# A decoder step's gate and up projections as seven half-size products, the down projection as a stage of its own

## The reference, cut to what matters

```python
D_FF = ((8 * D_MODEL + 767) // 768) * 256        # 5632
...
    hf = _rmsnorm(x, lp['norm_ffn_g'])
    x = x + (jax.nn.silu(hf @ lp['w_gate']) * (hf @ lp['w_up'])) @ lp['w_down']
...
y_prompt = _rmsnorm(xp, final_norm_g)
```

## Time and profile before

| | |
|---|---|
| median of 3 runs | 3788.56 us (3786.82 to 3789.76) |
| the profiled execution | 3790.81 us, span 3789.1 us |
| busy: TensorE (PE) / DVE / ACT / POOL | 92% / 42% / 25% / 2% of the span |
| TensorE's granted clock, mean | 0.965 of full speed |
| feed-forward stage, from co's end to its last matmul | 2218.5 to 3767.8 us |

### The profile page before, as it was taken

How to read it: one execution, slowest core, us unless ns; L and a number is a source line. 1 busy time by engine, 2 the same in 40 slices (tenths; PEclk the granted TensorE clock), 3 DMA queues, 4 the chain that set the end, 5 groups by cost and what they waited for, 6 DMA issues and landing times. The chain is left out here.

```text
span 3789.1 us, 80680 instructions
## 1 busy us (share of the span) xinstructions
PE 3485.2 (92%) x34315; PEld 3316.3 (88%) x34315; DVE 1591.5 (42%) x2387; ACT 958.4 (25%) x1224; POOL 61.5 (2%) x86
## 2 busy tenths in 40 slices
PE   8999999776688779899989999999999999999997
PEld 8899999544577777899957999999999999999997
DVE  4222444445666666433213344344343333333335
ACT  4111111226343534223113232211211211211213
POOL 0000000000011000000000000000000000000000
PEclk9999999888899999999999999999999999999999
DMA  4798222793000345322273222222222222222222
GB/s 174 278 351 323 97 89 90 297 380 147 23 0 0 124 169 193 118 89 78 96 319 141 99 78 90 90 90 98 81 97 94 86 94 90 90 90 90 90 94 86
DMA packets 97289, 492.70 MB, mean 130 GB/s; under 512 B 11025, under 2 KB 15378, under 8 KB 60994
## 3 DMA queue, kind: packets, MB, share of 16 engines
q1 hardware_dynamic: 92146, 472.67, 33.6%
q0 software_dynamic: 4944, 17.08, 1.2%
HBM read 470.25 MB, written 19.45 MB: 129 GB/s over the span
## 5 line engine op out<-in xcount | busy, mean ns | idle before, releaser
L2228 PE MATMUL ps<-hf_hi,whi_f 128*128 128x260 f32 x2816 | 569.6, 283 | 18.7 <-DVE bulk L2207 7.8
L2228 PE MATMUL ps<-hf_hi,wlo_f 128*128 128x260 f32 x2816 | 569.4, 284 | 0.0
L2228 PE MATMUL ps<-hf_lo,whi_f 128*128 128x260 f32 x2816 | 568.6, 284 | 0.0
L179 ACT ACTIVATE whi_f<-raw 128x2048 fp32r<-128x2048 f32 x132 | 252.7, 1915 | 959.6 <-PE ps L2228 958.5
L2228 PEld LDWEIGHTS ps<-hf_hi,whi_f 128*128 128x128 f32 x2816 | 436.3, 189 | 20.8 <-issue 11.9
L2228 PEld LDWEIGHTS ps<-hf_hi,wlo_f 128*128 128x128 f32 x2816 | 436.2, 189 | 0.0
L2228 PEld LDWEIGHTS ps<-hf_lo,whi_f 128*128 128x128 f32 x2816 | 435.1, 189 | 0.0
L183 DVE TENSOR_TENSOR wlo_f<-raw,whi_f 128x2048 fp32r<-128x2048 f32 x132 | 302.6, 2292 | 148.1 <-ACT whi_f L179 148.1
L2228 PE MATMUL ps<-hid_hi,whi_f 128*128 128x260 f32 x1408 | 284.1, 283 | 0.1
L2228 PE MATMUL ps<-hid_hi,wlo_f 128*128 128x260 f32 x1408 | 283.3, 283 | 0.0
L2228 PE MATMUL ps<-hid_lo,whi_f 128*128 128x260 f32 x1408 | 281.9, 281 | 0.0
(11 more groups left out here) (377 smaller groups left out, 4661.1 us busy)
## 6 DMA issues: line engine op xcount, KB each, us to landing
raw<-w SPq DMA_DIRECT2D x262, 1024.0 KB, 4.8
bulk<-kc SPq DMA_DIRECT2D x128, 512.0 KB, 6.3
page_ring<-vc SPq DMA_DIRECT2D x128, 512.0 KB, 6.0
mem_ring<-mkc SPq DMA_DIRECT2D x8, 2048.0 KB, 18.8
mem_ring<-mvc SPq DMA_DIRECT2D x8, 2048.0 KB, 11.5
qkv<-ev_a POOLq DMA_DIRECT2D x24, 260.0 KB, 2.3
qkv_head<-qkv SPq DMA_DIRECT2D x8, 780.0 KB, 7.6
bulk<-xt SPq DMA_DIRECT2D x4, 1040.0 KB, 11.1
```

The lines of the kernel that those rows point to most:

```text
L179: act.activation(whi[:, u, :], raw[:, u, :], ACT.Copy).then_inc(whi_done, 1)
L2228: mm = pe.matmul(ps[:, 2 * u + s, 0:m], wt[:, wslot, kcol:kcol + 128], t[:, k, a:a + m], start=(first and wt is whi and t is th), stop=(la ...
```

## The change

Three things. First, gate and up of one hidden tile become one product of a 2 x 2 block matrix (rows gate and up, columns the two halves of the 2048 inputs) with a 2 x 2 block matrix of `x` (halves of the inputs, halves of the tokens), made by Strassen's scheme in Winograd's form: 7 products of 128 x 1024 by 1024 x 260 in place of 8. The sums of weight quarters that it needs are made on POOL for each of the 44 hidden tiles, in place in the weight buffer; the sums of `x` quarters are made once on DVE, and all seven `x` operands are split into hi and lo once. The results are put together from the seven products on DVE, with two copies out of PSUM on ACT. Second, each hidden tile is written to DRAM by SP; the down projection becomes a stage of its own with 64 weight blocks (4 passes over the 16 output tiles, with 12, 12, 12 and 8 hidden tiles), which loads and splits the hidden tiles again. `x` is written to DRAM during `co` and read back for it, since the Strassen sums overwrite it. Third, in the attention, `place` moves from the beginning of its turn into the turn before.

```diff
@@ attention: place
-                                if i == 0:
-                                    place(t, hh)
+                                if i == 2 and hh == 0:
+                                    place(t, 1)
+                                elif i == 2 and not final:
+                                    place(t + 1, 0)
...
@@ co: x to DRAM
+                    for k in range(KT):
+                        pool.wait_ge(out_done, c0 + k + 3)
+                        if k >= 2:
+                            pool.wait_ge(x_kept[k % 2], 16 * (k // 2))
+                        pool.dma_start(xsp[k, :, :], x[:, k, :]).then_inc(x_kept[k % 2], 16)
...
@@ gate and up, for hidden tile b of turn t
+            operand = [b11, b21, b12, b22, b22, b11, b21]
+            BANK = (0, 1, 2, 3, 0, 1, 2)
...
+                            pool.tensor_tensor(t0, a21, a22, ALU.add).then_inc(s_made, 1)
+                            pool.wait_ge(s_made, count(t, b, 4, 1))
+                            pool.tensor_tensor(a21, a11, a21, ALU.subtract).then_inc(s_made, 1)
+                            pool.wait_ge(wlo_done, count(t, b, NP, lo0 + 1))
+                            pool.wait_ge(s_made, count(t, b, 4, 2))
+                            pool.tensor_tensor(a11, t0, a11, ALU.subtract).then_inc(s_made, 1)
+                            pool.wait_ge(wlo_done, count(t, b, NP, lo0 + 2))
+                            pool.wait_ge(s_made, count(t, b, 4, 3))
+                            pool.tensor_tensor(a12, a12, a11, ALU.subtract).then_inc(s_made, 1)
...
+                            hi(t, b, 6)
+                            more = not (last and b == 3)
+                            if more:
+                                hi(t, b + 1, 0)
+                            act.wait_ge(E, at(t, b, "z"))
+                            act.activation(sg, z, ACT.Sigmoid).then_inc(sig_done, 1)
+                            if more:
+                                for p in (1, 2, 3):
+                                    hi(t, b + 1, p)
...
+                    def lo(t, b, p):
+                        to = slot(is_first(t, b), p)
+                        dve.wait_ge(whi_done, count(t, b, NP, hi0 + p + 1))
+                        dve.tensor_tensor(to[:, 1, :], quarter(b, p), to[:, 0, :].bitcast(f32), ALU.subtract).then_inc(wlo_done, 1)
...
+                    dve.tensor_tensor(b12, b12, b11, ALU.subtract).then_inc(t_made, 1)
+                    lo(0, 0, 0)
+                    x_lo(0)
...
+                        for n, (wn, xs) in enumerate(((0, xh), (0, xl), (1, xh))):
...
+                            for k in range(QK):
+                                mm = pe.matmul(ps[:, 4 * (b % 2) + BANK[p], 0:HALF], to[:, wn, k * 128:k * 128 + 128], xs[:, p, k, :],
+                                               start=(n == 0 and k == 0), stop=(n == 2 and k == QK - 1))
...
@@ down, a second block of instruction streams
+            HEAD = 3
...
+                        sp.dma_start(bulk[:, KT:KT + HEAD, :], hid[k0:k0 + HEAD, :, :].rearrange("k p n -> p k n")).then_inc(h_in[0], 16)
+                        sp.dma_start(bulk[:, KT + HEAD:KT + n, :], hid[k0 + HEAD:k0 + n, :, :].rearrange("k p n -> p k n"))\
...
+                    for c in range(4):
+                        pe.wait_ge(hl_done, MADE_BY[c + 1] if c else 1)
+                        down(c, c * KT, 0, c == 0)
+                        down(c, c * KT + 1, 1, False)
+                        with pe.Fori(1, KT // 2) as t:
+                            for u in range(2):
+                                down(c, t * 2 + (c * KT + u), u, False)
```

More of the change, by code:

```diff
@@ L37 @@
 FFC = D_FF // 512
+HID = D_FF // 128
 LAM_INIT = 0.8 - 0.6 * math.exp(-0.3 * 0)
@@ L231, in project @@
                     squared=None, tail=None, paged=None, dve_first=None, beside=None, dve_begins=None,
-                    block=None, soft=None):
+                    block=None, soft=None, kept=None):
             j0 = jobs[0]
@@ new lines, in decoder_kernel @@
+        late.close()
+        hid = nc.dram_tensor("hidden", (HID, 128, TOK), f32, kind="Internal").ap()
+        QK = KT // 2
+        QW = QK * 128
+        NP = 7
+        j0 = jobs[0]
+        assert j0 % 2 == 0 and FF0 % 2 == 0 and HID % 2 == 0
+        hi0 = lo0 = FF0
+        pe0 = FF0 + 2
+        raw0 = 16 * (FF0 // 2) + 16
+        s_made, cut, E, sig_done = sem("s_made"), sem("product_copied"), sem("hidden_steps"), sem("sig_done")
+        h_out = [sem("h_out0"), sem("h_out1")]
+        xh_done, xl_done, t_made, scaled = sem("xh_done"), sem("xl_done"), sem("t_made"), sem("x_scaled")
@@ new lines, in decoder_kernel, with count @@
+        ssq_done, ms_done, rms_done = [sem(f"ff_{y}") for y in ("ssq", "ms", "rms")]
+        fin_pe, fin_gain, fin_act, fin_dve, fin_out = [sem(f"fin_{y}") for y in ("pe", "gain", "act", "dve", "out")]
+        s0_ = squares.turn(KT)
+        def count(t, b, per, n):
+            return t * (4 * per) + (per * b + n)
+        STEPS = ("g0", "s2", "a", "g1", "z", "s3", "u1", "q", "qr", "u0", "h")
+        PASSES = [(0, 3), (3, 6), (6, 9), (9, FFC)]
+        TILES = [4 * (e - a) for a, e in PASSES]
@@ new lines, in _, with body @@
+                    turns_of(sp, body)
+                @block.gpsimd
+                def _(pool):
+                    def body(t, last):
+                        for b in range(4):
+                            r = blocks[b % 2]
+                            a11, a12, a21, a22 = r[:, 0, 0:QW], r[:, 0, QW:], r[:, 1, 0:QW], r[:, 1, QW:]
+                            landed(pool, t, b)
+                            if not is_first(t, b):
+                                pool.wait_ge(wlo_done, count(t, b, NP, lo0 - NP + 3))
+                                pool.wait_ge(s_made, count(t, b, 4, 0))
+                            pool.tensor_tensor(t0, a21, a22, ALU.add).then_inc(s_made, 1)
[7 more added lines that the diff above has]
+                            pool.tensor_tensor(a12, a12, a11, ALU.subtract).then_inc(s_made, 1)
+                    turns_of(pool, body)
@@ L2125, in _ @@
                 def _(act):
[L2126 to L2149, removed]
@@ new lines, in _ @@
+                    for i in range(NB):
+                        if i + 2 < NB:
+                            hi(i + 2)
+                        c, k = i // KT + 1, i % KT - 3
+                        if c < 4 and 0 <= k < TILES[c]:
+                            hidden_hi(c, k)
+                        if c == 4:
+                            k = i % KT
+                            act.wait_ge(out_done, j0 + i + 3)
+                            squares.square(act, x[:, k, :], k % 2, s0_ + k)
+                            act.activation(x[:, k, :], x[:, k, :], ACT.Copy, scale=V("g_final", k)).then_inc(fin_gain, 1)
@@ L2224, in _ @@
                 def _(pe):
-                    def product(k, kcol, u, wslot, th, tl, first, last):
-                        for wt, t in ((whi, th), (whi, tl), (wlo, th)):
-                            for s, (a, m) in enumerate(SPANS):
-                                mm = pe.matmul(ps[:, 2 * u + s, 0:m], wt[:, wslot, kcol:kcol + 128], t[:, k, a:a + m],
-                                               start=(first and wt is whi and t is th), stop=(last and wt is wlo))
-                        return mm
```

447 lines of the change are left out of this document (327 added, 120 removed).

## The result

The change makes the kernel slower: 3886.11 us (median of four runs, 3883.86 to 3890.37) against 3788.56, a ratio of 1.026 with a 95% interval of 1.024 to 1.028. The forecast was 3866, the range 3750 to 3965, "slower" had 0.70. The profiled execution took 3890.4 us (span 3888.7), 99.6 more than before's.

A forecast was written before the change was run, and what follows sets the result against it. TensorE, busy 92% of the span, was taken as the bound of the kernel before. Profiled 3790.8 + 81 (feed-forward) - 4 (attention) = 3868 us, 3866 us as a median; range 3750 to 3965.

The forecast's parts named there:

- The mechanism: Gate and up: DVE instructions with two SBUF operands stand still while POOL computes, so POOL's 9.4 us adds to DVE's 14.9.
- no run shows yet: Gate and up: whether POOL in turn waits behind a DVE instruction was left open, as no row showed it.
- Matmuls, 127 us less: Gate and up: seven half-size products in place of eight, 1,056 fewer matmuls at 0.1203 us each.
- The period, 24.2 us: Gate and up, per hidden tile: DVE's and POOL's time plus DVE's wait, less overlap, against TensorE's 20.2 us.
- The wait for ACT: Gate and up: DVE waits 1.8 us a tile because ACT makes the next tile's second hi part only after the sigmoid.
- Rival 3, the clock: Gate and up: pauses lower TensorE's clock, 2.2 us more a tile, 26.4 us in all, 3960 us; chance 0.13.
- Start of the stage: Gate and up's first tile: product five starts at 48 us and the tile's last product ends at 57 us.
- Gate and up: Whole gate and up stage: 57 + 43 x 24.2 + 1 = 1,098 us.
- To the down stage: Between gate and up and down: change of blocks, loading and splitting hidden tiles, and TensorE's half clock, 13 us.
- Down: Down stage: 508 us of matmuls, 7 for loop turns, 4 for loads ahead of weight blocks, 519 us.
- At no cost: In co: writing `x` to DRAM and ACT's gain on it lie under other work; uncovered they would cost 16 x 0.7 us.
- Attention, 4 us less: Attention: part of TensorE's 16.9 us of waits for `place` comes back, 4 us, between 0 and 12.

The follow-up runs named there:

- E1: The change with POOL's four sums of each tile made over 16 columns in place of 1,024; 3678.5 us, one run.
- E4: The change with DVE making the four sums from the second tile on, POOL only the first tile's; 3689.07 us, ratio to before 0.9725.
- E7: The change with POOL's sums made over 16 columns and the other 1,008 columns filled with zeros by POOL; 3678.0 us, one run.
- E3: The change with weight slots going round evenly, each product taking the slot of the product four before; 3814.65 us, ratio to before 1.006.
- E8: The kernel before with only the change's attention part, `place` a head earlier; 3784.84 us, ratio to before 0.9993.
- E5: The change with ACT making the next tile's hi part 1 before the sigmoid instead of behind it; 3788.86 us, ratio to before 0.9997.
- E6: The change with weight slots going round evenly and hi part 1 ahead of the sigmoid, sums still on POOL; 3741.59 us, ratio to before 0.9881.

## Why the prediction was right, and where it was off

*The mechanism.* "A DVE instruction with both operands in SBUF stands still while POOL computes", read from one row, carried the sign. E1 and E4 take the sums from POOL and win 208 and 197 us; E7 shows that it is the reading. My row for an operand in PSUM stood beside copies on POOL; line 2349, 0.41 us inside a sum, is the comparison that was missing. The Trainium skill (page "SBUF — State Buffer", "Who interferes with whom") says the same and also that a GpSimd instruction that only writes does not contend: E7 agrees (0.70 us beside a fill of 0.94). What "no run shows yet", POOL behind DVE, is shown: 2.72 us for 2.40, and 1.25 for 0.22 in E7.

*Matmuls, 127 us less.* 1,056 matmuls fewer, as said; a tile of 168 takes 20.11 us in E1 and E4, forecast 20.2.

*The period, 24.2 us.* Measured 24.8 (43 tiles between the first tile's end at 2277.3 and the stage's last matmul at 3344.4). The parts were off in both directions. DVE without POOL is 13.4 us, not 14.9: a lo part of 1.22 us lets the next start after 1.14, so the gaps that I added are overlaps. POOL's four sums take 10.2 us, not 9.4 (2.40 unheld where I took 2.34 from the earlier trace rows, and 2.7 for two that wait for DVE). Of these, some 8.0 us are hold, where I had 8.8. The wait for ACT is 1.65, forecast 1.8. That sum is 23.1 us, the tile of E3. It was rightly built and is not what bounds the change: **the step that failed is that a tile is a sum over one engine.** It is a ring through a weight slot, 0.7 us longer, and, since the ring goes through TensorE, the clock counts in it too, 0.9 us. 23.1 + 0.7 + 0.9 = 24.7. That 24.2 came so near to 24.8 is partly luck: the list was put 1.1 us too long, and the ring and its clock, 1.6 us, were not in it.

*Rival 3, the clock.* I gave it 2.2 us a tile as a case of its own. It came in part: in this turn two tiles in four, 2.4 and 1.35 us.

*Start of the stage.* 57 us forecast, 58.1 measured (2219.2 to 2277.3). The fifth product (product 4) starts at 47.0 us (2266.22), forecast 48.

*Gate and up:* 1,098 forecast, 1,125 measured. *To the down stage:* 13 forecast, 8.9 measured. *Down:* 519 forecast, 515 measured. (The 2.4 us of half clock that I put into the first lie, as measured here, in the second.) The feed-forward is 1,649 us against 1,549, +100 where I had +81; nothing of the loss lies in the down stage or the trip through DRAM.

*At no cost:* the next stage's first matmul starts at 2219.22 us, 0.6 later than before, behind a change of blocks of 4.38 us, where the earlier trace rows have 2.5; co's matmuls themselves end no later. The cover held.

*Attention, 4 us less.* Measured 3 less, within 6 less and 1 more, not to be told from none. "DVE's own `place` moves to where it waits for the exponentials" was costed at nothing; the softmax weights behind it then kept TensorE 11 us (E8).

So 3866 became 3886: 27 us more in gate and up, 8 less behind it, and 1 more for the attention by E8's median, which can't be told from none.

## What to carry to other kernels

Before work goes to POOL, list what DVE does beside it: in the loop of these runs every DVE instruction with both operands in SBUF that started inside a sum stood until the sum had ended, so a sum cost DVE 2.0 us on POOL and 1.22 us in its own list. Once the engines' sums are made, follow one buffer slot round (who frees it, who fills it, who waits for that): here the longest such ring set the period, and because it went through TensorE it also paid for TensorE's clock. And when you take one bound away, work out the next: here 24.7 (ring and clock), 23.1 (DVE's list), 21.4 (without ACT's wait), 20.1 us (TensorE) stood close behind one another, and E5, at 22.1 to 23.7 us, is where the change broke even (forecast 22.5).

## What the runs showed of the hardware

- TensorE's granted clock fell to its lower level (0.50 from 2740.75 to 2746.00 us, 1.2 GHz) after a pause of 3.42 us that in the tile before had left it at 1.00 (2716.90 to 2722.00). It fell after some pauses of 2.7 us (E3) and 1.8 us (E5) too, and after none of those of 1.0 us in 193 us of E6 (clock 1.00). What decides between the two levels no run here shows.
- POOL's sum of two full operands took 2.40 us for 1,024 columns, a fill of 1,008 columns 0.94 us (E7).
- DVE's instructions overlap at their ends: behind a lo part of 1.21 us the next one starts after 1.14 us (2740.56 and 2741.70).
